# Sparse attention: items in the order of token halves, half of the second key search between the first items, four-head output banks

## The chip, the cores and the metric

The kernel runs on one core of a Trainium2 chip. The metric is the device time of one execution in microseconds (us). The core has TensorE (matrix products, PE), VectorE (DVE), ScalarE (ACT), GpSimd (POOL) and SyncE (SP, which here only issues DMAs), each with its own queue of instructions, worked off in order. They meet on semaphores. TensorE writes to eight PSUM banks of 128 x 512 float32; the others read them from there.

## The reference

Two model blocks run one after the other over 256 tokens of width 1024, all in float32. The first block is a pair of layers (recurrent mixers, then full attention, each with a feed-forward part). The second has, beside a convolution and a pooling branch, a sparse attention with compressed keys, and then a mixture of 32 experts. The sparse attention is what the change touches, cut to its core:

```python
topk = min(TOPK_MAX, S // 4)                       # 64 keys of 256
q_abs = einsum('bthd,khd->bthk', q, w_uk)          # 8 heads, latent width 128
score = einsum('bqhs,bqh->bqs', relu(qi @ ki), wi) * idx_scale
score = where(key_chunk <= query_chunk, score, -inf)   # chunks of 64 tokens
_, idx = top_k(score, topk)                        # the same keys for all heads
logits = einsum('bqhc,bqkc->bqhk', q_abs, ckv[idx]) * att_scale
p = softmax(where(valid, logits, -inf))
ctx = einsum('bqhk,bqkc->bqhc', p, ckv[idx])       # then times w_uv, into y_att
mix = concat([y_conv, y_att, y_pool]) @ w_out
```

## The kernel before, in words

Tokens are split into two halves of 128 (t = 0 and 1), which lie on the 128 partitions. Queries of half t see (t + 1) key blocks of 128: one for the first half, two for the second. Instead of gathering the chosen keys, the kernel builds a bias (0 for a chosen key, -1e30 for the rest) and runs the attention densely over the key blocks.

**The search for the best keys** is on VectorE (`best_keys(t)`, lines 2172 to 2179). It scales and masks the scores into `work` (line 2174), then runs eight rounds of MAX8 (line 2177, the eight greatest values of each row) and MATCH_REPLACE8 (line 2178, which strikes them out), and last turns what was struck out into the bias `bias2` (line 2179). `step` is a wait of VectorE for its own last instruction. Both halves are searched before the attention starts, t = 0 first.

**The attention** works on 16 items, each one head and one half of the tokens. Item i is head i // 2, half i % 2: the halves alternate. An item passes through the engines like this, each engine with its own loop over i, written out by hand:

- TensorE (`attend`, lines 1327 to 1345): the score matmul of item i (line 1334), into a bank of its own; LAG = 4 items later the transposes of its probabilities (line 1341, carried out at line 796), into another bank; and after the transposes of an odd item of head h, the output products of head h - 1 (`out_of`, line 1356), both halves. Two heads share a bank.
- VectorE (`attend`, lines 2034 to 2054): scale and add the bias while reading the bank (line 2044), the negative maximum (line 2047), and two items later the reciprocal of the sum (line 2052) and the product with it (line 2054).
- ScalarE (`attend`, lines 2495 to 2519): the exponential of item i with its row sum (line 2502), then for item i - 4 the copy of the transposed probabilities to `probT2` (line 2514), one of four buffers. It first waits until the output products of the item that had the buffer are done. After items 5, 9 and 13 it also copies a full output bank to `ctxT` (line 2287), and the fourth at the end.

The same functions serve the full attention of the first block ("att"), which the change leaves as it is.

**Banks** are taken in a fixed rotation over the eight (`Banks.take`, line 133); a bank that is held is left out of it until it is released. A taken bank makes TensorE wait until its last content was read. During the sparse attention two banks are held by `out_early(0, 0)` and `out_early(0, 1)`, the parts of the output projection that don't need the attention (lines 1494 to 1509), issued just ahead of it; `out_early(1, 0)` stands right behind it in TensorE's queue.

**What follows:** the products with w_uv (line 1525, "yatt"), whose end frees the slot of the attention's weights and lets SyncE load the first five expert weight units (lines 2677 to 2679); the rest of the output projection, the router, the choice of experts, and the expert stage, whose 96 weight units of 2 MB each pass through eight slots; a slot is loaded anew when TensorE has used it (line 2673).

## Time and profile before

| | us |
|---|---|
| median of 3 runs | 1467.24 |
| lowest and highest run | 1466.57, 1469.61 |
| the profiled execution | 1473.01 |
| its span (first to last instruction) | 1471.2 |
| TensorE busy (matmul) | 1223.2 |
| VectorE busy | 609.4 |
| ScalarE busy | 445.2 |
| first item of the sparse attention begins (line 2044) | 937.73 |
| its last probabilities are ready | 957.49 |
| first expert weights are requested | 965.97 |
| first expert matmul | 1009.85 |

The times in the timeline are microseconds from the span's start, in the profiled execution. A row of the timeline gives the start, the duration, the engine, the line, the operation, what it writes and reads, how many instructions were merged, and in brackets how long the engine had been idle before it and what ended the wait. A float32 matmul shows as two records, so `x2` is one product of one key block. "PEld" are the weight loads beside TensorE's matmuls. The granted clock is TensorE's, as a share of 2.4 GHz. In a row of the stages the count behind a busy time (x12) is its number of instructions.

### The profile page before, as it was taken

To read this page: it belongs to the slowest core of one execution; us is meant where nothing else is said; L and a number is where in the kernel's file an instruction comes from. 1 tells how busy PE (TensorE), PEld (TensorE's weight loads), DVE (VectorE), ACT (ScalarE), POOL (GpSimd) and SP (SyncE) were. 2 spreads that over 40 slices of the span, in tenths; PEclk is the share of its full clock that TensorE was granted. 3 is DMA by queue.
4 is the path that set the end of the run, shared out by engine and by line. 5 is a ranking of instruction groups with operands and counts; after the bars stand their busy time and mean duration, and the time that the engine had idled before them with its cause. 6 is when DMAs were issued, how large, how long until landed. Compare 5 with 4: busy or idle time off the path is not lost.

```text
span 1471.2 us, 18072 instructions
## 1 busy us (share of the span) xinstructions
PE 1223.2 (83%) x7648; PEld 898.1 (61%) x7648; DVE 609.4 (41%) x971; ACT 445.2 (30%) x685; POOL 16.2 (1%) x32
## 2 busy tenths in 40 slices
PE   5999999999999998999999999798464665646637
PEld 5998886699787787599888786554121321312213
DVE  4588423577543666366643548822100100101002
ACT  4662330344333675353432523532010010000002
POOL 2000000000000000000000000000000000000000
PEclk9999999999999999999999989998787878868878
DMA  8362559355464544144455634076999999999995
GB/s 265 123 215 72 199 203 340 125 176 193 160 216 144 195 174 168 57 172 172 172 181 190 190 114 145 1 296 267 428 429 429 429 429 428 428 428 428 429 425 238
DMA packets 98060, 362.98 MB, mean 247 GB/s; under 512 B 7193, under 2 KB 10612, under 8 KB 86084
## 3 DMA queue, kind: packets, MB, share of 16 engines
q1 hardware_dynamic: 95952, 357.70, 62.9%
q0 software_dynamic: 1680, 4.10, 1.0%
q8 instruction: 55, 0.90, 0.2%
q10 hardware_dynamic: 356, 0.13, 0.0%
q14 instruction: 17, 0.14, 0.0%
HBM read 360.87 MB, written 1.05 MB: 246 GB/s over the span
## 4 chain that ended last, share of the span: by engine, by line
PE 59%; DMA 22%; DVE 8%; issue 2%; ACT 2%; SPq 1%; DVEq 0%; ACTq 0%
PE bank L855 33%; DMA arena<-in_exp_w 21%; PE bank L628 7%; PE bank L969 3%; PE bank L796 2%; DVE arena L2123 2%; PE bank L1189 2%; PE bank L827 2%; PE bank L1181 1%; PE bank L1490 1%; PE bank L1162 1%; PE bank L837 1%; SPq L2673 1%; DVE low_w L1636 1%; DMA ring<-in_w_out_ar 1%
## 5 line engine op out<-in xcount | busy, mean ns | idle before, releaser
L628 PE MATMUL bank<-arena 128*32 128x512 f32 x944 | 198.7, 706 | 97.0 <-DMA arena<-in_exp_w 92.1
L1636 DVE TENSOR_TENSOR low_w<-ring,split_high 128x2048 fp32r<-128x2048 f32 x84 | 189.7, 2289 | 114.9 <-ACT split_high L2302 114.8
L855 PE MATMUL bank<-turned_high,low_w 128*128 128x256 f32 x720 | 204.4, 284 | 0.0
L2302 ACT ACTIVATE split_high<-ring 128x2048 fp32r<-128x2048 f32 x84 | 157.6, 1912 | 146.5 <-DMA ring<-in_w_down 60.0
L628 PE MATMUL bank<-ring,arena 128*32 128x512 f32 x528 | 94.0, 694 | 86.6 <-DMA arena<-in_exp_w 86.6
L628 PEld LDWEIGHTS bank<-arena 128*32 128x32 f32 x944 | 51.4, 127 | 167.7 <-issue 167.7
L855 PE MATMUL bank<-turned_high,split_high 128*128 128x256 f32 x512 | 145.9, 285 | 3.0 <-DVE turned_low L1651 3.0
L855 PE MATMUL bank<-turned_low,split_high 128*128 128x256 f32 x512 | 144.9, 283 | 0.0
L855 PEld LDWEIGHTS bank<-turned_high,low_w 128*128 128x128 f32 x720 | 139.0, 193 | 0.0
L733 DVE TENSOR_TENSOR arena<-arena,bank 128x512 f32<-128x512 f32 x8 | 5.5, 689 | 300.1 <-PE bank L628 300.1
L2287 ACT ACTIVATE arena<-bank 128x512 f32<-128x512 f32 x110 | 62.3, 596 | 207.2 <-PE bank L855 135.6
L628 PEld LDWEIGHTS bank<-ring,arena 128*32 128x32 f32 x528 | 26.5, 125 | 150.6 <-issue 150.6
L855 PE MATMUL bank<-split_high,actT_high 128*128 128x512 f32 x256 | 101.3, 396 | 5.3 <-DVE actT_low_late L1964 5.3
L855 PEld LDWEIGHTS bank<-turned_high,split_high 128*128 128x128 f32 x512 | 98.3, 192 | 3.9 <-issue 3.9
L855 PE MATMUL bank<-low_w,actT_high 128*128 128x512 f32 x256 | 100.6, 393 | 0.0
L855 PEld LDWEIGHTS bank<-turned_low,split_high 128*128 128x128 f32 x512 | 98.3, 192 | 0.5 <-issue 0.5
L768 ACT ACTIVATE arena<-bank 128x512 f32<-128x512 f32 x8 | 4.8, 597 | 258.4 <-PE bank L628 258.4
L855 PE MATMUL bank<-split_high,actT_low 128*128 128x512 f32 x192 | 75.9, 395 | 0.0
L855 PE MATMUL bank<-low_w,turned_high 128*128 128x512 f32 x176 | 69.1, 393 | 0.0
L855 PE MATMUL bank<-split_high,turned_high 128*128 128x512 f32 x160 | 64.1, 400 | 3.6 <-DVE low_w L1636 2.1
L855 PE MATMUL bank<-turned_high,split_high_in 128*128 128x256 f32 x208 | 60.6, 291 | 4.0 <-DVE low_w L1636 4.0
L855 PE MATMUL bank<-split_high,turned_low 128*128 128x512 f32 x160 | 63.0, 394 | 0.0
(424 smaller groups left out, 1967.6 us busy)
## 6 DMA issues: line engine op xcount, KB each, us to landing
arena<-in_exp_w SPq DMA_DIRECT2D x59, 2048.0 KB, 22.9
ring<-in_exp_w SPq DMA_DIRECT2D x33, 2048.0 KB, 20.7
ring<-in_w_up SPq DMA_DIRECT2D x16, 2048.0 KB, 8.6
ring<-in_w_down SPq DMA_DIRECT2D x16, 2048.0 KB, 7.9
ring<-in_mod_w SPq DMA_DIRECT2D x12, 2048.0 KB, 8.0
ring<-in_w_in_ar SPq DMA_DIRECT2D x7, 2048.0 KB, 8.6
ring<-in_w_qkv SPq DMA_DIRECT2D x6, 2048.0 KB, 8.0
ring<-in_ple_gate SPq DMA_DIRECT2D x4, 2048.0 KB, 7.9
```

Source lines behind the costliest of these rows:

```text
L628: last = mm(mb[bank][strip(e), :], act[:, k, strip(e)], w[e][:, k, cols], start=(k == 0), stop=(k == n_k - 1), skip_group_check=True)
L796: last = nc.tensor.transpose(dst, src, ident[0:src.shape[0], 0:src.shape[0]])
L827: last = mm(bank.ap[:, i * S:(i + 1) * S], w[:, k, m:m + P], act[:, k, :], start=(k == 0), stop=(k == kcs - 1))
L837: last = mm(bank.ap[:, 0:n], act[:, k, t * P:(t + 1) * P], w[:, k, 0:n], start=(k == 0), stop=(k == kcs - 1))
L855: last = mm(dst, *pair, start=(start and i == 0), stop=(stop and i == 2))
L969: last = mm(bank.ap[:, :], hT3[:, k, t * P:(t + 1) * P], w[:, k, :], start=(k == 0), stop=(k == KC - 1), skip_group_check=True)
L1162: last = mm(mod_bank.ap[strip, :], cond3[:, k, at:at + STRIP], w[:, k, :], start=(c == 0 and k < 4), stop=(c == MOD_UNITS - 1 and k >= 4), ...
L1189: last = mm(bank.ap[:, i * P:(i + 1) * P], a_inv[:, 4 * g + i, :], invT[:, 4 * g + i, :], start=True, stop=True)
L1636: v.tensor_tensor(low_of(name, s), half_of(slot(name), name, s), high_of(name, s).bitcast(F32), ALU.subtract).then_inc(sem("split_low"), 1)
L2123: last = v.scalar_tensor_tensor(conv_acc[:, c, :], src, conv_col[:, c, k:k + 1], conv_acc[:, c, :], ALU.mult, ALU.add)
L2287: s.activation(dst, src, func, scale=scale).then_inc(bank.freed, 1)
L2302: nc.scalar.activation(high_of(name, s), half_of(slot(name), name, s), ACT.Copy)\
```

## The change

- The items of the sparse attention are taken in the order of token halves: items 0 to 7 are the eight heads of half 0 (one key block each), items 8 to 15 those of half 1 (two key blocks each).
- VectorE searches half 0 as before, then masks half 1 and runs four of its eight rounds. The other four stand one each between the maximum and the reciprocal of items 0 to 3, and the bias of half 1 behind the last of them.
- TensorE issues the output product of one item behind the transposes of the next one, in place of a head's two behind the next head's. An output bank holds four heads of one half, in place of two heads of both; it is held (left out of the rotation) from its first product to its last.
- ScalarE copies an output bank, now four heads of one half of `ctxT`, ahead of the transposed probabilities of items 5, 9 and 13 in place of behind them, and the fourth at the end. It waits for single items' output products.

```diff
--- before.py
+++ after.py
@@ -1344,6 +1344,42 @@
                             out_of(tag, h - 1, value, probsT)
                 out_of(tag, HEADS - 1, value, probsT)
 
+            def attend_halves(tag, items_q, items_k, value, landed_sem, probs, probsT):
+
+                n = 2 * HEADS
+
+                def out_item(j):
+                    t, h = divmod(j, HEADS)
+                    if h % 4 == 0:
+                        open_bank[tag] = banks.hold(pe, tag, "o", j // 4)
+                    bank = open_bank[tag]
+                    banks.wait_read(pe, tag, "pT", j)
+                    for k in range(t + 1):
+                        last = mm(bank.ap[:, (h % 4) * P:(h % 4 + 1) * P], value(h, k), probsT[:, j % 4, k, :],
+                                  start=(k == 0), stop=(k == t))
+                    if h % 4 == 3:
+                        last.then_inc(bank.full, 1)
+                        banks.release(tag, "o", j // 4)
+                    else:
+                        last.then_inc(sem(tag + "_out"), 1)
+
+                for i in range(n + LAG):
+                    if i < n:
+                        t, h = divmod(i, HEADS)
+                        bank = banks.take(pe, tag, "s", i)
+                        mm(bank.ap[:, 0:(t + 1) * P], items_q(h)[:, t * P:(t + 1) * P], items_k(h)[:, 0:(t + 1) * P],
+                           start=True, stop=True).then_inc(bank.full, 1)
+                    if i >= LAG:
+                        i2 = i - LAG
+                        t = i2 // HEADS
+                        bank = banks.take(pe, tag, "pT", i2)
+                        pe.wait_ge(sem(landed_sem), i2 + 1)
+                        transposes([(bank.ap[:, k * P:(k + 1) * P], probs[:, i2 % 8, k * P:(k + 1) * P])
+                                    for k in range(t + 1)], bank)
+                        if i2:
+                            out_item(i2 - 1)
+                out_item(n - 1)
+
             open_bank = {}
 
             def out_of(tag, h, value, probsT):
@@ -1510,7 +1546,7 @@
             for g in range(4):
                 banks.wait_read(pe, "qabs", g)
             banks.wait_read(pe, "ckvT")
-            attend("dsa", lambda h: q_abs[:, h, :], lambda h: ckvT, lambda h, k: ckv_tok[:, k, :],
+            attend_halves("dsa", lambda h: q_abs[:, h, :], lambda h: ckvT, lambda h, k: ckv_tok[:, k, :],
                    "dsa_prob", prob2, probT2)
             out_early(1, 0)
             for c in range(4):
@@ -2031,11 +2067,15 @@
                     .then_inc(sem("rotated"), 1)
                 dve.wait_ge(sem("rotated"), q + 1)
 
-            def attend(tag, scale, mask, probs, extra=None):
+            def attend(tag, scale, mask, probs, first_half_first=False, beside=None):
                 n = 2 * HEADS
+
+                def half_of_item(i):
+                    return i // HEADS if first_half_first else i % 2
+
                 for i in range(n + 2):
                     if i < n:
-                        t = i % 2
+                        t = half_of_item(i)
                         bank = banks.read(dve, tag, "s", i)
                         if i >= 8:
                             banks.read(dve, tag, "pT", i - 8)
@@ -2045,9 +2085,11 @@
                             .then_inc(bank.freed, 1)
                         banks.wait_read(dve, tag, "s", i)
                         v.tensor_reduce(nmax[:, i:i + 1], part, AX.X, ALU.max, negate=True).then_inc(sem(tag + "_max"), 1)
+                    if beside:
+                        beside(i)
                     if i >= 2:
                         i2 = i - 2
-                        t = i2 % 2
+                        t = half_of_item(i2)
                         dve.wait_ge(sem(tag + "_exp"), i2 + 1)
                         step(v.reciprocal(rinv[:, i2:i2 + 1], rsum[:, i2:i2 + 1]))
                         part = probs[:, i2 % 8, 0:(t + 1) * P]
@@ -2169,14 +2211,25 @@
                     last.then_inc(sem("rel_used"), 1)
                     dve.wait_ge(sem("rel_used"), 4 * t + g + 1)
 
-            def best_keys(t):
+            def mask_keys(t):
                 n = (t + 1) * P
                 step(v.scalar_tensor_tensor(work[:, t, 0:n], score[:, t, 0:n], float(512) ** -0.5,
                                             c_("allowed", t * S, t * S + n), ALU.mult, ALU.add))
-                for r in range(8):
-                    step(v.max(top8, work[:, t, 0:n]))
-                    step(v.match_replace(work[:, t, 0:n], top8, work[:, t, 0:n], -3e38))
+
+            def next_best(t):
+                n = (t + 1) * P
+                step(v.max(top8, work[:, t, 0:n]))
+                step(v.match_replace(work[:, t, 0:n], top8, work[:, t, 0:n], -3e38))
+
+            def key_bias(t):
+                n = (t + 1) * P
                 step(v.tensor_scalar(bias2[:, t, 0:n], work[:, t, 0:n], -2e38, NEG, ALU.is_gt, ALU.mult))
+
+            def search_beside(i):
+                if i < 4:
+                    next_best(1)
+                if i == 3:
+                    key_bias(1)
 
             add_scores(0)
             bank = banks.read(dve, "cvar")
@@ -2185,9 +2238,14 @@
             dve.wait_ge(sem("conv_root"), 1)
             step(v.reciprocal(conv_m[:, 0, :], conv_m[:, 0, :]))
             v.tensor_tensor(conv_acc, conv_acc, mid(conv_m[:, 0, :], 2), ALU.mult).then_inc(sem("conv_normed"), 1)
-            for t in range(NT):
-                best_keys(t)
-            attend("dsa", 64.0 ** -0.5, lambda t: bias2[:, t, 0:(t + 1) * P], prob2)
+            mask_keys(0)
+            for r in range(8):
+                next_best(0)
+            key_bias(0)
+            mask_keys(1)
+            for r in range(4):
+                next_best(1)
+            attend("dsa", 64.0 ** -0.5, lambda t: bias2[:, t, 0:(t + 1) * P], prob2, True, search_beside)
             for n in range(2):
                 for t in range(NT):
                     bank = banks.read(dve, "w_out2", n, t)
@@ -2518,6 +2576,35 @@
                             evacuate(dst[:, 2 * c:2 * c + 2, :], ACT.Copy, tag, "o", c)
                 evacuate(dst[:, 6:8, :], ACT.Copy, tag, "o", 3)
 
+            def attend_halves(tag, probs, probsT, dst):
+                n = 2 * HEADS
+
+                def take_out(c):
+                    evacuate(dst[:, 4 * (c % 2):4 * (c % 2) + 4, c // 2 * P:(c // 2 + 1) * P], ACT.Copy, tag, "o", c)
+
+                for i in range(n + LAG):
+                    if i < n:
+                        t = i // HEADS
+                        part = probs[:, i % 8, 0:(t + 1) * P]
+                        act.wait_ge(sem(tag + "_max"), i + 1)
+                        s.activation(part, part, ACT.Exp, bias=nmax[:, i:i + 1], accum_out=rsum[:, i:i + 1])\
+                            .then_inc(sem(tag + "_exp"), 1)
+                    if i >= LAG:
+                        i2 = i - LAG
+                        t = i2 // HEADS
+                        if i2 >= 4:
+                            last_item = i2 - 4
+                            if last_item % 4 == 3:
+                                banks.read(act, tag, "o", last_item // 4)
+                            else:
+                                act.wait_ge(sem(tag + "_out"), last_item + 1 - (last_item + 1) // 4)
+                        if i2 >= 5 and (i2 - 5) % 4 == 0:
+                            take_out((i2 - 5) // 4)
+                        bank = banks.read(act, tag, "pT", i2)
+                        s.activation(probsT[:, i2 % 4, 0:t + 1, :], blocks(bank.ap[:, 0:(t + 1) * P], t + 1), ACT.Copy)\
+                            .then_inc(bank.freed, 1)
+                take_out(3)
+
             feed_forward(0)
             act.wait_ge(sem("ple_added"), 2 * NT)
             norm(3, blocks(page(6, 2), NT))
@@ -2606,7 +2693,7 @@
                 bank = banks.read(act, "qabs", g)
                 h0 = 4 * (g % 2) + g // 2
                 s.activation(q_abs[:, h0:h0 + 3:2, :], blocks(bank.ap, 2), ACT.Copy).then_inc(bank.freed, 1)
-            attend("dsa", prob2, probT2, ctxT)
+            attend_halves("dsa", prob2, probT2, ctxT)
             for g in range(2):
                 rows_ = slice(64 * g, 64 * g + 64)
                 for c in range(2):
```

## Rows read from the trace of the kernel before

**Rows 1.** The page: its head, and part 4, the chain that ended last.

```profile
span 1471.2 us, 18072 instructions
...
PE 59%; DMA 22%; DVE 8%; issue 2%; ACT 2%; SPq 1%; DVEq 0%; ACTq 0%
```

**Rows 2.** Stages: length; busy us of PE, PEld, DVE, ACT, POOL; PEclk; DMA share; GB/s.

```profile
940.00:944.00 4.00, 3.82 (x12) 2.48 (x13) 3.76 (x16) 2.30 (x11) 0.00 (x0) 0.50 0.00 0
...
946.00:958.00 12.00, 8.26 (x62) 7.13 (x62) 9.11 (x36) 7.78 (x30) 0.00 (x0) 1.00 0.01 3
...
1008.00:1020.00 12.00, 10.15 (x76) 3.14 (x80) 0.00 (x0) 0.60 (x1) 0.00 (x0) 0.74 0.02 5
...
1025.00:1440.00 415.00, 236.33 (x1666) 95.49 (x1662) 34.99 (x98) 22.75 (x45) 0.00 (x0) 0.79 1.01 428
```

**Rows 3.** Timeline, VectorE, second half's search: start us, us, engine, line, operation.

```profile
929.53 0.43 DVE L2177 MAX8 small<-arena 128x8 f32<-128x256 f32 x1
...
937.40 0.29 DVE L2179 TENSOR_SCALAR arena<-arena 128x256 f32<-128x256 f32 x1
```

**Rows 4.** Timeline, TensorE around the first score matmuls.

```profile
927.15 7.13 PE L1490 MATMUL bank<-ring,hT 128*128 128x512 f32 x16
...
934.12 1.69 PE L1334 MATMUL bank<-arena 128*128 128x128 f32 x10
...
940.18 0.45 PE L796 MATMUL bank<-const,arena 128*128 128x128 f32 x1 [4.36 <-DVE arena L2054]
```

**Rows 5.** Timeline, VectorE: item 2 (narrow) and item 3 (wide).

```profile
939.04 0.28 DVE L2044 SCALAR_TENSOR_TENSOR arena<-bank,arena 128x128 f32<-128x128 f32 x1
...
939.56 0.15 DVE L2052 RECIPROCAL small<-small 128x1 f32<-128x1 f32 x1
...
939.95 0.42 DVE L2044 SCALAR_TENSOR_TENSOR arena<-bank,arena 128x256 f32<-128x256 f32 x1
...
940.74 0.15 DVE L2052 RECIPROCAL small<-small 128x1 f32<-128x1 f32 x1
...
941.19 0.28 DVE L2044 SCALAR_TENSOR_TENSOR arena<-bank,arena 128x128 f32<-128x128 f32 x1
```

**Rows 6.** Timeline, from item 9's start to item 11's.

```profile
946.91 0.42 DVE L2044 SCALAR_TENSOR_TENSOR arena<-bank,arena 128x256 f32<-128x256 f32 x1
...
947.81 0.51 ACT L2502 ACTIVATE arena<-arena,small 128x256 f32<-128x256 f32 x1 [0.52 <-DVE small L2047]
...
948.32 0.36 ACT L2514 ACTIVATE arena<-bank 128x256 f32<-128x256 f32 x1
...
948.58 0.58 ACT L2287 ACTIVATE arena<-bank 128x512 f32<-128x512 f32 x1
...
949.39 0.60 PE L1334 MATMUL bank<-arena 128*128 128x256 f32 x2
...
950.02 0.42 DVE L2044 SCALAR_TENSOR_TENSOR arena<-bank,arena 128x256 f32<-128x256 f32 x1 [0.87 <-PE bank L1334]
```

**Rows 7.** Timeline, item 8 (narrow), its score at the low clock.

```profile
945.32 0.64 PE L1334 MATMUL bank<-arena 128*128 128x128 f32 x2
...
945.99 0.29 DVE L2044 SCALAR_TENSOR_TENSOR arena<-bank,arena 128x128 f32<-128x128 f32 x1 [0.39 <-PE bank L1334]
...
946.64 0.40 ACT L2502 ACTIVATE arena<-arena,small 128x128 f32<-128x128 f32 x1 [0.60 <-DVE small L2047]
...
947.04 0.26 ACT L2514 ACTIVATE arena<-bank 128x128 f32<-128x128 f32 x1
```

**Rows 8.** Timeline, item 15 and the end of the attention.

```profile
955.30 0.42 DVE L2044 SCALAR_TENSOR_TENSOR arena<-bank,arena 128x256 f32<-128x256 f32 x1 [0.87 <-PE bank L1334]
...
958.03 1.68 PE L1356 MATMUL bank<-arena 128*128 128x128 f32 x12
...
959.54 3.60 PE L1490 MATMUL bank<-ring,hT 128*128 128x512 f32 x8
...
965.97 2.42 SPq L2673 DMA_DIRECT2D arena<-in_exp_w  x4
```

## The prediction

> **What bounds the kernel now.** I read the page first: the span is 1471.2 us, and the chain that ended last is TensorE for 59% and DMA for 22% [rows 1]. The stage table shows why both matter. From 1025 us on, the DMA engines are full at 428 GB/s with the expert weights, so that stretch has a fixed length; from 1008 to 1020 us they carry nothing, because all eight weight slots are full and the first group has not been consumed [rows 2]. So the end is set by when routing and the first expert matmuls happen, and every microsecond by which the sparse attention ends sooner or later goes through to the end one to one. The first expert loads wait too for the last use of its weights: they go out at 965.97 [rows 8]. Both move together, so nothing absorbs a delay.
>
> Inside the attention, VectorE is the pacemaker. It searches the keys of the second half in eight rounds of 0.98 us, from 929.53 to the bias at 937.40 [rows 3], and then runs 16 items. An item with one key block (narrow) takes 0.91 us from start to start, one with two (wide) 1.24; up to the reciprocal, the part that items 0 and 1 consist of, it is 0.52 and 0.79 [rows 5]. The first 15 would need 0.52 + 0.79 + 7 x 0.91 + 6 x 1.24 = 15.1 us; item 15 starts 955.30 - 937.73 = 17.57 us after item 0 (937.40 + 0.29 + 0.04) [rows 3, 8]. The missing 2.4 us are three waits for a score matmul: 0.39 us at 945.99, and 0.87 at 950.02 and at item 15 [rows 6 to 8].
>
> **Search moved.** The same 16 + 16 search instructions run, in the same order for each half, and each is one long dependent chain with no hole that other work could fill: rounds are worth 0.98 us wherever they stand. VectorE's total is unchanged. What the move does is reach the first item four rounds and the bias earlier: 937.73 - 4 x 0.98 - 0.33 = 933.47. But TensorE is then still in its 16 early output matmuls and starts the first score only at 934.12 [rows 4]. With 0.45 us for a narrow score (0.67 at the low clock [rows 7], less 0.11 for each of its two records at the full one) item 0 starts at 934.57: a new wait of **+1.1 us**, which the rounds covered before. It can't be nothing (the score's start is fixed by TensorE's own queue) and at most 1.3.
>
> **Order of items.** Narrow items come first. Item 4 starts after 2 x 0.52 + 2 x 0.91 of items and 4.27 of search: 941.70. Without any wait item 15 would start at 934.57 + 4.27 + 15.06 = 953.90, 1.4 us before the 955.30 of now (15.06: two of 0.52, six of 0.91, two of 0.79 + 0.39 = 1.18, five of 1.24). It will not, for a wait that the new code adds. Before, the output products of a head ran one head behind, so that score k+3 waited for what follows the exponential of item k, and only every second one. Now TensorE's order is score i, transposes of i-4, output of item i-5; the last waits for ScalarE's copy of the transposes i-5, and ScalarE issues that copy behind the exponential of item i-1. Score i+1 is queued behind it. So **score k+2 waits for the exponential of item k**, a loop over two items:
> - Narrow, low clock: item start to exponential 0.65, to copy 0.40 [rows 7]; copy 0.26 and 0.1 to TensorE; two output records, 0.126 each by the twelve between 958.03 and 959.54 [rows 8], doubled, 0.50; score 0.67. Sum 2.58 where VectorE needs 1.82.
> - Wide, full clock: 0.90 to the exponential, 0.51 to the copy [rows 6], 0.46 copy and hand-over, output 0.50 (0.25 and 0.36 for a narrow item), score 0.63: 3.00, or 2.65, where VectorE needs 2.48.
> - At items 9 and 13 ScalarE takes the output bank first (0.58 [rows 6], 0.5 start to start), and now ahead of the copy: 3.15 and 3.50.
>
> The clock: it is 0.50 from 940 to 944 and 1.00 from 946 [rows 2]; before it fell TensorE had stood idle from 935.8 to 940.18 [rows 4]. In the new order its five first scores end near 935.2 and the first probability comes near 939.5, so the same idle gap and the same fall; I take the rise at item 8, a little later, since TensorE is less dense. Adding up: item 6 starts at 941.70 + 2.58 = 944.28 (0.76 late), item 8 at 946.9 (between 946.6 with the clock up and 947.3 with it down; 0.8 late), 10, 11, 13, 14 and 15 lose 0.29, 0.44, 0.17, 0.35 and 0.67. Sum of waits 3.5: item 15 starts at 957.4, **+2.1 us** against 955.30. This term holds the 1.1 of the start and the 2.4 us of old waits that go. Bounds: -1.4 (no wait at all) and +3.0 (low clock until item 12).
>
> **Output banks and the end.** Four-head banks, still four, same 0.6 us evacuations. The bank rotation is what changes: two banks are held by the early output, and one more while it is filled, so five rotate. Counting takes through, transposes of item 13 land on the bank of output 2 (items 8 to 11). That bank is full after output 11, which waits for the copy of transposes 11, which stands behind exponential 15. From item 15's start: copy at +1.41, output 11 from +1.87 to +2.37, evacuation to about +3.05, and then TensorE still has transposes 13, 14, 15 and outputs 12 to 15: 6 + 16 = 22 records at 0.112 to 0.126 = 2.5 to 2.8 us. The early output of (1, 0) starts at +5.6 to +5.9; now it starts at 959.54 - 955.30 = +4.24 [rows 8], because transposes ran ahead of that evacuation. **+1.3 us**, the lower end, since the second-last outputs already overlap. Bounds: -0.1 (22 records for 23, were there no bank wait) and +1.7. Behind it the 3.6 us of early output cover the last evacuation as before.
>
> The head products, routing and expert stage are untouched, and a later last use of the weights only moves the loads. SP's queue and the one of GpSimd issue nothing new. Semaphore counts (15 increments in place of 4) cost no time on an engine that waits anyway. Sum: 2.1 + 1.3 = 3.4 us. The profiled execution took 1473.0 (span 1471.2 and 1.8 around it) and the median of the runs is 1467.24; the stage has no part that differs between runs, so I add the same 3.4 us to the median: **1470.6**.
>
> A rule weighed: from 940 to 946 TensorE works at 1.2 GHz and from 946 at 2.4, though it still pauses (8.3 of 12 us busy) [rows 2]. The Trainium skill, TensorE: Matmul & The Clock Gate, section "A second HAM failure mode: psum-queue depth-cycling", says that short idle pauses of a TensorE cycling through PSUM banks can make its clock swing between the levels. By that rule the new, more evenly broken queue could stay at 1.2 GHz for most of the stage. The trace of before agrees only in part: with 3.7 us of pauses in the 12 after 946 its clock did not fall.
>
> **Rivals.**
> - *The clock stays low longer.* TensorE's pauses are shorter but more frequent. Two-item loop for a wide item over a narrow one at 1.2 GHz: 0.90 + 0.51 + 0.36 + 0.50 + 1.06 (0.63 and twice the 0.22 that a narrow score loses) = 3.3. Low until item 12: item 15 at 958.3, +3.0, and the end +1.4: 1467.2 + 4.4 = 1471.6; through the end, 22 records double, 1474.4. For: 940 to 946 is such a time; against: the clock rose in the midst of the same kind of work.
> - *Only one of the two delays is there.* ScalarE's copy reaches TensorE in time (loop below 1.82 and 2.48), or output 11 is early enough to free the bank: about +1.5, 1468.8, no change. Against: the loop's terms are all rows.
> - *Faster.* VectorE alone is the pacemaker and the old bank waits simply go. It decides if an output product can start within about 0.9 us of the item's start: then item 15 starts at 953.9, and the end is 1.4 + 0.1 earlier: 1465.7. For: the two 0.87 us waits come from a bank that is reused six takes later, and the held bank ends that; against: evacuation still stands in ScalarE's queue ahead of work that scores need.
> - *It does not do what it says:* the search's second half lies "between" items but on the same engine, so nothing is hidden; the rest (start +1.1, old waits -2.4 or kept) gives -1.3 to +1.1. Its middle is 1467.2; it shares the mark of "only one delay".
>
> **Chances.** Forecast (both delays, +2.0 to +4.6, 1469.2 to 1471.8) 0.55; clock low longer 0.12; one or no delay near zero net 0.21; faster 0.12. A change of under 0.2% (2.9 us) can't be told from none here: the three runs before lie 3.0 us apart. The forecast sits just above that line, so about 0.6 of it counts as slower: 0.55 x 0.6 + 0.12 + a rest of 0.02 = 0.47 slower. Of "faster" even the bound of all waits gone is 1.5 us, so only 0.07 goes past the line, for what I did not see; 0.46 for no change. Range 1466.0 to 1473.0: it takes in the small cases near 1467 and 1468.8, most of the low-clock case, and leaves out the faster end and the low clock to the end.
>
> **What would show it.** Item 0 of the second search waits about 1.1 us for a score; VectorE's waits for scores grow from 2.1 us in 3 places to about 4.5 in eight or more, on even and odd items; item 15 starts near 957.4; TensorE waits about 0.7 us for ScalarE's last-but-one output evacuation before transposes 13; the early output (1, 0) starts near 963, and the first expert load near 969.4; expert stage unchanged in length. Wrong if the first expert load goes out before 967, if outputs wait for no copy, or if the stage moved and the end did not.

## The result and the profile after

| | before | after |
|---|---|---|
| median, us (20 runs each) | 1469.03 | 1474.11 |
| ratio after / before | | 1.0035 (95%: 1.0027 to 1.0042) |
| profiled execution: time, span | 1473.01, 1471.2 | 1472.86, 1471.1 |

The change makes the kernel slower by 0.35%, that is by 5.1 us (4.0 to 6.2). One of the 20 runs of after took 1843 us at a mean granted clock of 0.66, against 0.92 in the others, and is left out of the ratio. The two profiled executions don't show this in their spans: the one of after reached the attention 4.0 us earlier, in code that is the same, and such differences between executions are as large as the effect. So I read the stage, not the span. "Stage" is from VectorE's scaling of the convolution, the 128x512 product just ahead of the first key search, to the first expert load. This is one profile for each kernel:

| us | before | after | difference | forecast |
|---|---|---|---|---|
| scaling of the convolution to item 0 | 15.59 | 12.47 | -3.12 | -3.2 |
| item 0 to item 15 | 17.57 | 23.70 | +6.13 | +5.3 |
| item 15 to early output (1, 0) | 4.24 | 6.22 | +1.98 | +1.3 |
| early output (1, 0) to first expert load | 6.43 | 6.42 | 0 | 0 |
| **stage** | 43.83 | 48.81 | **+4.98** | +3.4 |

The first two lines belong together, since 4.27 us of search moved from the one to the other. The stage's 5.0 us agree with the 5.1 of the time, as well as single profiles can show it: from the first expert load to the end of the span the two profiles have 505.2 us before and 504.1 after, in code that the change leaves as it is.

VectorE's timeline of after, the first score wait and the items that waited most (the columns as in [rows 5]). It answers to [rows 3 to 5]:

```profile
929.05 0.41 DVE L2222 MATCH_REPLACE8 arena<-small,arena 128x256 f32<-128x256 f32 x1
...
930.64 0.29 DVE L2084 SCALAR_TENSOR_TENSOR arena<-bank,arena 128x128 f32<-128x128 f32 x1 [1.18 <-PE bank L1370]
...
931.17 0.42 DVE L2221 MAX8 small<-arena 128x8 f32<-128x256 f32 x1
...
940.44 0.29 DVE L2084 SCALAR_TENSOR_TENSOR arena<-bank,arena 128x128 f32<-128x128 f32 x1 [0.76 <-PE bank L1370]
...
943.48 0.42 DVE L2084 SCALAR_TENSOR_TENSOR arena<-bank,arena 128x256 f32<-128x256 f32 x1 [0.97 <-PE bank L1370]
...
954.34 0.42 DVE L2084 SCALAR_TENSOR_TENSOR arena<-bank,arena 128x256 f32<-128x256 f32 x1 [0.53 <-PE bank L1370]
```

Item 0 waits 1.18 us: the search that used to cover TensorE's early output matmuls is gone from there. A round stands between two instructions that had nothing to wait for. Items 6, 8, 9, 11, 14 and 15 wait for their scores. The waits of after, from 925 to 967 us (engine, line, what it waited for: us, times, longest), where before had 2.1 us in three places:

```profile
DVE arena L2084 <- PE bank L1370: 4.5, 7, 1.2
...
PE bank L1358 <- ACT arena L2604: 2.8, 5, 0.9
...
PE bank L796 <- ACT arena L2345: 1.9, 3, 0.8
```

The reason is one step back, in TensorE's and ScalarE's rows around items 13 and 15. They answer to [rows 6]:

```profile
950.83 0.42 DVE L2084 SCALAR_TENSOR_TENSOR arena<-bank,arena 128x256 f32<-128x256 f32 x1
...
951.75 0.51 ACT L2590 ACTIVATE arena<-arena,small 128x256 f32<-128x256 f32 x1 [0.57 <-DVE small L2087]
...
952.25 0.58 ACT L2345 ACTIVATE arena<-bank 128x512 f32<-128x512 f32 x1
...
952.73 0.37 ACT L2604 ACTIVATE arena<-bank 128x256 f32<-128x256 f32 x1
...
952.88 0.44 PE L796 MATMUL bank<-const,arena 128*128 128x128 f32 x2 [0.45 <-ACT arena L2345]
...
953.16 0.71 PE L1358 MATMUL bank<-arena 128*128 128x128 f32 x4
...
953.70 0.60 PE L1370 MATMUL bank<-arena 128*128 128x256 f32 x2
```

Read it from item 13 on: exponential at 951.75, then the output bank (L2345) at 952.25, then the copy (L2604) at 952.73, TensorE's transposes at 952.88, output at 953.16, and only behind it the score of item 15 (L1370) at 953.70. VectorE takes it at 954.34, 3.51 us after item 13's start at 950.83. Two wide items need 2.48.

The end of the attention, which answers to [rows 8]:

```profile
955.25 0.51 ACT L2590 ACTIVATE arena<-arena,small 128x256 f32<-128x256 f32 x1 [1.00 <-DVE small L2087]
...
955.76 0.64 ACT L2604 ACTIVATE arena<-bank 128x256 f32<-128x256 f32 x2
...
956.17 0.71 PE L1358 MATMUL bank<-arena 128*128 128x128 f32 x4 [0.94 <-ACT arena L2604]
...
956.98 0.60 ACT L2345 ACTIVATE arena<-bank 128x512 f32<-128x512 f32 x1 [0.59 <-PE bank L1358]
...
957.63 0.44 PE L796 MATMUL bank<-const,arena 128*128 128x128 f32 x2 [0.75 <-ACT arena L2345]
...
960.56 3.60 PE L1526 MATMUL bank<-ring,hT 128*128 128x512 f32 x8
...
966.98 2.61 SPq L2760 DMA_DIRECT2D arena<-in_exp_w  x4
```

The copy of transposes 11 stands behind exponential 15; output 11 follows at 956.17, its bank is evacuated from 956.98, and TensorE's next transposes (item 13) wait 0.75 us for it, with four items of output still to do.

The granted clock of after, and the expert stretch, in the same columns as [rows 2]:

```profile
935.00:945.00 10.00, 7.01 (x24) 5.26 (x24) 7.39 (x32) 3.72 (x17) 0.00 (x0) 0.51 0.00 0
...
946.00:958.00 12.00, 8.11 (x49) 5.97 (x48) 8.60 (x29) 7.49 (x25) 0.00 (x0) 1.00 0.01 2
...
1025.00:1440.00 415.00, 240.41 (x1666) 96.54 (x1662) 35.01 (x98) 22.73 (x45) 0.00 (x0) 0.78 1.01 428
```

The clock is at half from 935 to 945 us; before, it was from 940 to 946. The expert stretch still runs at 428 GB/s, and from the first expert matmul to the end of the span the profiles have 461.4 us before and 460.3 after.

### The profile page after: what moved, and what is told of

Read it like the earlier page. It is cut to its first block, busy times and chain, and to the rows that moved or that the text cites. A ratio compares the mean times of both kernels' runs of the same rounds, so it can differ in the third digit from the quotient of the medians.

```text
span 1471.1 us, 18076 instructions
## 1 busy us (share of the span) xinstructions
PE 1224.2 (83%) x7648; PEld 897.1 (61%) x7648; DVE 609.8 (41%) x971; ACT 445.2 (30%) x685; POOL 16.1 (1%) x32
## 4 chain that ended last, share of the span: by engine, by line
PE 60%; DMA 22%; DVE 7%; ACT 2%; issue 2%; SPq 1%; DVEq 0%; ACTq 0%
PE bank L855 32%; DMA arena<-in_exp_w 21%; PE bank L628 7%; PE bank L969 3%; PE bank L796 2%; PE bank L1526 2%; DVE arena L2165 2%; PE bank L827 2%; PE bank L1189 2%; PE bank L1162 2%; PE bank L1181 1%; PE bank L837 1%; SPq L2760 1%; DVE low_w L1672 1%; DVE arena L2084 1%
## 5 line engine op out<-in xcount | busy, mean ns | idle before, releaser
L628 PE MATMUL bank<-arena 128*32 128x512 f32 x944 | 201.8, 713 | 94.6 <-DMA arena<-in_exp_w 90.2
L2345 ACT ACTIVATE arena<-bank 128x512 f32<-128x512 f32 x110 | 62.2, 596 | 207.7 <-PE bank L855 135.7
```

Of the source, the lines that this page charges most:

```text
L628: last = mm(mb[bank][strip(e), :], act[:, k, strip(e)], w[e][:, k, cols], start=(k == 0), stop=(k == n_k - 1), skip_group_check=True)
L2345: s.activation(dst, src, func, scale=scale).then_inc(bank.freed, 1)
```

## The experiments

All are variants of after but one. "Time" is the ratio of the runs to those of before on the same chip, with its 95% interval; "first matmul" is from the first expert load to the first expert matmul. Stage, waits and first matmul come from one profile of each kernel, the time from 11 or 12 runs of it (20 for after), so the two need not agree to the microsecond. The time of x4 lies lower than its stage says (1.4 us above before would be 1.0010), and no run shows why.

| kernel | stage, us | VectorE's score waits behind item 0 | first matmul | time |
|---|---|---|---|---|
| before | 43.83 | 2.13 | 43.9 | |
| after | 48.81 | 3.29 | 43.8 | 1.0035 (1.0027 to 1.0042) |
| x1 search ahead | 47.28 | 3.05 | 47.3 | 1.0025 (1.0013 to 1.0037) |
| x2 copy first | 44.01 | 0.41 | 45.5 | 1.0016 (1.0003 to 1.0030) |
| x3 evacuation last | 49.05 | 3.58 | 44.0 | 1.0034 (1.0021 to 1.0048) |
| x4 output later | 45.23 | 0.92 | 43.9 | 0.9998 (0.9989 to 1.0007) |
| y1 turn banks | 48.82 | 3.26 | 43.9 | 1.0043 (1.0030 to 1.0056) |
| y2 gap busy | 48.82 | 3.35 | 43.8 | 1.0031 (1.0012 to 1.0050) |
| y3 combined | 43.19 | 0.49 | 43.8 | 0.9998 (0.9982 to 1.0014) |
| y4 combined, gap used | 40.60 | 1.21 | 44.3 | 0.9980 (0.9965 to 0.9994) |
| z1 ahead, busy | 48.22 | 2.69 | 44.1 | 1.0020 (1.0008 to 1.0031) |
| z2 before, gap used | 43.14 | 3.47 | 44.0 | 1.0003 (0.9990 to 1.0016) |
| z3 gap used, search between | 40.92 | 1.33 | 45.6 | 0.9990 (0.9979 to 1.0000) |
| z4 ahead, real filler | 48.27 | 2.69 | 44.0 | 1.0028 (1.0016 to 1.0040) |

### x1: the whole search ahead of the items

```diff
-            for r in range(4):
+            for r in range(8):
                 next_best(1)
-            attend("dsa", ..., prob2, True, search_beside)
+            key_bias(1)
+            attend("dsa", ..., prob2, True)
```

> Stage = from VectorE's scaling of the convolution (the 128x512 product just ahead of the first key search) to the first expert load: 43.8 us before, 48.8 after. Here the new order and banks stay, and all eight rounds of the second search run ahead of the attention. Theory A (score k+2 waits for what follows exponential k; late bank at the end; 1.2 us wait for the first score): only the 1.2 us of the start go, the rest stays: stage 47.6, time 3.9 us above before. Theory C (the search between the items is what costs, since it delays first exponentials and lengthens TensorE's idle time): stage below 46. Theory D (the move hides something): stage above 48.8.

Measured: stage 47.28, 1.53 us less than after (theory A: 1.2), and 3.45 more than before. Theory A holds: the move of the search costs the wait for the first score and hides nothing. Theory C is out: with the search back in its place most of the loss stays, in items that wait as before (0.76, 0.89, 0.30, 0.27, 0.30, 0.53) and the same 6.2 us at the end.

### x2: ScalarE copies ahead of its exponentials

```diff
                 for i in range(n + LAG):
+                    if i >= LAG:
+                        ...            # copy of item i - LAG and output bank
                     if i < n:
                         ...            # exponential of item i
-                    if i >= LAG:
-                        ...
```

> ScalarE copies the transposes (and output bank) of item i-4 ahead of the exponential of item i; all else as after. Theory A: this cuts both the two-item loop and the end (copy 11 no longer behind exponential 15). VectorE's waits for scores fall from 3.5 us behind the first one to about 1.5 (those at the low clock), the end from 6.2 us behind item 15's start to about 4.5; stage about 45, time 0.5 to 1.5 above before. Theory B (TensorE at the low clock with one product per item is simply too slow): waits stay above 3, stage 47.5 or more.

Measured: stage 44.01; behind item 0 only item 8 still waits (0.41 us, where 1.5 in all was expected), and the end is 5.23 us behind item 15's start (expected 4.5). So this one swap takes back 4.8 of the 5.0 us, 3.8 between items 0 and 15 and 1.0 at the end; I had expected 3.8 in all. This is the cleanest sign for the loop, since TensorE's work, order and banks are untouched. The clock is not quite: it was at half for some 7 us here (934 to 940) and for 10 in after, so that item 9's score ran at the full clock. But item 6 lies in the low stretch in both and waits 0.76 us in after and not at all here; and in y2 below the low stretch is 7 us too and the stage as long as after's. ScalarE's rows of this kernel, around item 13:

```profile
946.72 0.58 ACT L2345 ACTIVATE arena<-bank 128x512 f32<-128x512 f32 x1
...
947.20 0.37 ACT L2598 ACTIVATE arena<-bank 128x256 f32<-128x256 f32 x1
...
947.47 0.50 ACT L2604 ACTIVATE arena<-arena,small 128x256 f32<-128x256 f32 x1
...
949.05 0.42 DVE L2084 SCALAR_TENSOR_TENSOR arena<-bank,arena 128x256 f32<-128x256 f32 x1
```

The output bank (946.72) and the copy (947.20) now run before the exponential of item 13 (947.47), which waits for nothing on VectorE's side, and item 15 starts at 949.05 without a wait. In the time the gain is smaller than in the stage (ratio 1.0016); in the profile TensorE's clock fell early in the routing stretch, of which more below.

### x3: output banks 0 and 1 behind the copies

```diff
-                        if i2 >= 5 and (i2 - 5) % 4 == 0:
+                        if i2 == 13:
                             take_out((i2 - 5) // 4)
                         ...            # copy of item i2
+                        if i2 in (5, 9):
+                            take_out((i2 - 5) // 4)
```

> ScalarE takes output banks 0 and 1 behind the copies of items 5 and 9 as before, in place of ahead of them; bank 2 stays ahead. Theory A: items 11 and 15 wait up to 0.5 us less each: stage 48.0. Theory B: no difference (48.8).

Measured: 49.05, 0.24 more, where 48.0 was expected. This part of theory A fell. Items 11 and 15 wait 0.63 and 0.70 us, more than after's 0.51 and 0.53. The score needs both: the bank (the transposes of items 6 and 10 land on it) and the copy. Turning the two around makes the bank later by a copy.

### x4: output products one item later

```diff
-                        if i2:
-                            out_item(i2 - 1)
+                        if i2 >= 2:
+                            out_item(i2 - 2)
+                out_item(n - 2)
                 out_item(n - 1)
```

(and ScalarE takes an output bank at i2 = 6, 10, 14)

> TensorE issues the output product of item j behind the transposes of item j+2 (in place of j+1), and ScalarE takes an output bank one item later. Theory A: the loop becomes three items long and no longer binds; waits of VectorE for scores fall to about 1.6 us (low clock, and 0.4 for a bank at item 12), the end to about 5.4 us behind item 15's start; stage about 46, time 2 above before. Theory B: as TensorE does the same work, the waits stay: 48 or more.

Measured: 45.23 (theory A: about 46), waits 0.92 us in two places (item 8 at the low clock, item 12 for a bank), and 5.86 us at the end. Theory B expected 48 with the same work on TensorE. With x2 this settles the loop: it goes when either of its two links is given room, the product issued an item later or the copy ahead of the exponential.

### y1: banks of the x transposes

Behind the attention the new rotation gives the first transposes of x the bank of output part (1, 0), which VectorE has still to read. After, from TensorE's timeline:

```profile
980.99 0.69 DVE L2253 TENSOR_TENSOR arena<-bank,arena 128x512 f32<-128x512 f32 x1 [2.02 <-PE bank L1526]
...
981.73 1.09 PE L796 MATMUL bank<-const,x 128*128 128x128 f32 x8 [0.85 <-DVE arena L2253]
```

```diff
+            banks.at = 7
             turn_x(0, 0)
             turn_x(0, 1)
```

> As after, but the rotation is set so that the transposes of x behind the output projection take banks 0 and 1 again, as before the change (after, they take the bank of output part (1, 0), and TensorE waits 0.85 us for VectorE to read it). Stage = from VectorE's scaling of the convolution to the first expert load (43.8 before, 48.8 after); next stretch = from the first expert load to the one behind the last piece of the output projection (22.8 before, 23.85 after). Theory A (four places of loss, this one 1.1 us): stage 48.8 unchanged, next stretch 22.8, time about 1 us under after, 4 above before. Rival (that wait lies beside other work): next stretch falls, but the first expert matmul stays at 43.8 us behind the first load, and the time does not change.

Measured: the stretch to the eighth load falls from 23.85 to 22.78 us as expected, but the first expert matmul stays at 43.88 behind the first load and the time does not fall. The rival holds: this wait lies beside other work. What it lies beside is DMA. First expert matmuls of after and of y1:

```profile
1010.76 8.51 PE L628 MATMUL bank<-arena 128*32 128x512 f32 x64 [4.47 <-issue]
```

```profile
1009.20 8.49 PE L628 MATMUL bank<-arena 128*32 128x512 f32 x64 [5.66 <-issue]
```

The eighth load took 19.9 us from 990.83 in after, 21.1 from 988.10 in y1 and 21.0 from 988.75 in before, so it landed at 1010.7, 1009.2 and 1009.8; the matmuls began at 1010.76, 1009.20 and 1009.85. The eighth unit lands 43.8 to 43.9 us behind the first request in all three, and in x1 and x2 too (43.9 and 43.8), whatever routing does meanwhile. So the first matmul follows the first expert load, until routing gets later than that: in x1 the clock fell early in the routing stretch (the row below has length, busy us by engine, clock, DMA; before, it stayed at 1.00 there and was at 0.50 only from 991 to 997, 25 us behind the load), and the first matmul came 47.3 us behind the load; in x2, with the same fall, 45.5. That would explain why x2 gained less in time than in the stage, but only one profile of x2 shows it.

```profile
982.00:992.00 10.00, 9.55 (x36) 6.14 (x35) 0.40 (x1) 2.90 (x7) 0.00 (x0) 0.66 1.02 434
```

TensorE's wait in front of the first expert matmul is shown as "issue". In the code this matmul waits for its own four units (`group_products`), the first to be requested, and not for the eighth; that it starts as the eighth lands is what the profiles show, and why is open.

### y2, z1 and z4: TensorE kept busy in its gap

```diff
+                    if i == LAG:
+                        for _ in range(4):
+                            mm(mixed_bank[(0, 0)].ap[:, :], zeros, const[:, 0:512], start=False, stop=False,
+                               skip_group_check=True)
```

y2 is after with this, z1 is x1 with it; z4 is z1 with real values (features times output weights) into a bank of their own.

> As after, with four products of a zero matrix (added to a held bank, 3.6 us) in TensorE's idle gap between the first five scores and the first transposes; TensorE is then no longer idle for 4.4 us and its granted clock should stay at 1.00. Theory A (loop of two items, made longer by the low clock): VectorE's waits for scores behind the first fall from 3.3 us to about 1.6, those of items 6, 8, 9 nearly vanish, 11, 14, 15 stay; stage 48.8 to about 47. Rival (loop alone, the clock is no part of it): stage stays within 0.3 of 48.8.

> The version with the search ahead of the items (stage from VectorE's scaling of the convolution to the first expert load: 47.28) and four products of a zero matrix in TensorE's gap. In the version with the search between, the same filler did not hold the clock: it fell in the pauses of 1.7 and 0.9 us between the thin first items. If those pauses are the reason, the clock now stays at 1.00 to the end of the attention, VectorE's waits for scores fall from 3.05 us to about 2 (only the loop at the full clock), stage about 46.2. Rival (products of zeros do not count as activity): clock falls as before, stage 47.3.

> The same as the version with the search ahead and a filler of zeros in TensorE's gap (stage 48.2, granted clock low from 937 to 940 and again at the end of the attention), but the four filler products take real values (normed features times output weights) into a bank that nobody reads, with the rotation set back; same sizes, same number. If what the products hold matters to the granted clock, it stays at 1.00 from the gap to the end, VectorE's waits for scores are those of the loop at the full clock (about 2 us, against 2.7) and the stage is 45.7 to 46.4. If only time matters, all is as with zeros: 47.5 or more and a fall within 5 us of the filler's end.

Measured, y2: stage 48.82, nothing gained, and neither theory right about why. The filler ended at 935.8; the clock stayed at 1.00 until 940 and was then 0.51 to 0.50 until 946, so that items 6, 8 and 9 met it as before (0.77, 0.97, 0.22). The filler only moved the fall. z1 and z4 have dense first items, and the clock fell still (from 937 in z1, from 939.5 in z4), so that z1 ended above both values expected of it (46.2 and 47.3). The stages of z4 (length, busy us of PE, PEld, DVE, ACT, POOL, clock, DMA):

```profile
932.00:936.00 4.00, 3.93 (x13) 1.67 (x11) 3.71 (x14) 0.50 (x2) 0.00 (x0) 1.00 0.00 0
...
936.00:939.50 3.50, 1.18 (x7) 0.89 (x8) 3.22 (x16) 2.39 (x10) 0.00 (x0) 1.00 0.00 0
...
939.50:942.50 3.00, 3.00 (x13) 2.38 (x13) 1.98 (x9) 1.70 (x9) 0.00 (x0) 0.53 0.00 0
...
942.50:955.00 12.50, 9.26 (x51) 6.46 (x49) 9.98 (x34) 7.27 (x27) 0.00 (x0) 0.98 0.01 3
...
957.00:960.00 3.00, 3.00 (x15) 3.00 (x15) 0.00 (x0) 0.77 (x2) 0.00 (x0) 0.50 0.00 0
```

TensorE is busy 1.18 of the 3.5 us ahead of the fall. The low time is shorter than in x1, which brings 0.4 us in the items (waits 2.69 against 3.05), but the clock falls a second time at the end and costs 1.4 us there (item 15 to the early output 7.6 us against 6.2). Zeros and real values gave the same to 0.05 us. So the expectation that the gap of 4.4 us is what lowers the clock fell three times: without it the clock falls too, only later. Nor is it a single pause: from the filler to the fall z4 paused 1.09, 0.39 and 0.91 us, while y4 below paused 1.07, 0.39, 1.48 and 1.40 us and stayed at 1.00 through all items. What decides is open. And the loop costs its waits also at the full clock: items 10 to 15 of z4 wait 1.40 us at 0.98 to 1.00.

### y3 and y4: a version from the findings

y3 is x1, x2 and y1 together. y4 puts early output (1, 0), which stood behind the attention, into the gap as well:

```diff
+                    if i == LAG:
+                        out_early(1, 0)
...
-            out_early(1, 0)
```

> After, with the whole search ahead of the items, ScalarE's copies ahead of its exponentials, and the banks of the x transposes set back. Theory A: the single effects add: 48.8 less 1.5 (search) less 4.8 (copies) = stage 42.5, next stretch 22.8 at the full clock; 1.3 us below before, time 0 to 1.5 below before. Rival (waits overlap, so that single gains do not add): stage 43.5 or more.

> As the combined one, and the early part (1, 0) of the output projection (3.5 us of TensorE) is moved from behind the attention into TensorE's idle gap ahead of the first transposes. Theory A: the gap of 4.4 us shrinks to about 1, the clock stays at 1.00, and at the end only 0.8 us for the last output bank remains of the 3.5: stage 42.5 - 2.7 - 0.4 = about 39.5, time about 4 below before. Rival (three held banks starve the rotation): VectorE's waits grow by 2 us or more and the stage stays above 41.

Measured, y3: 43.19, 0.6 us below before, where 42.5 was expected. Of x1's 1.5 us only 0.8 came on top of x2. The time is that of before (0.9998). y4: 40.60, 3.2 us below before, and the time 0.9980 (0.9965 to 0.9994): faster than both kernels. The clock stayed at 1.00 (the expectation came true here, though not in y2, z1 and z4), and TensorE went from the last output product to the products with w_uv in 0.9 us:

```profile
941.38 0.49 PE L1358 MATMUL bank<-arena 128*128 128x128 f32 x2 [1.48 <-ACT arena L2348]
...
942.34 0.42 DVE L2086 SCALAR_TENSOR_TENSOR arena<-bank,arena 128x256 f32<-128x256 f32 x1 [0.56 <-PE bank L1370]
...
954.12 0.60 ACT L2348 ACTIVATE arena<-bank 128x512 f32<-128x512 f32 x1 [0.80 <-PE bank L1358]
...
954.98 2.83 PE L1562 MATMUL bank<-arena,ring 128*64 128x256 f32 x16 [0.89 <-ACT arena L2348]
...
957.84 0.34 SPq L2763 DMA_DIRECT2D arena<-in_exp_w  x1
```

Three held banks do cost: TensorE waited 1.48 us for output bank 0 and 1.40 for the next, and VectorE 0.56 and 0.65 us for scores. That is part of why the gain is 3.2 and not 4.3; the rest is y3's shortfall of 0.7.

### z2: the same use of the gap in the kernel before

> The kernel before, with the early part (1, 0) of the output projection in TensorE's gap ahead of the first transposes and the banks of the x transposes as they were; no item order, no four-head bank. If the gain of the best version so far (stage 40.6, against 43.8 before) comes from that move and not from the new order, this one reaches 40.5 to 41.5. If the held four-head banks and ScalarE's order are needed beside three held banks, VectorE's waits grow (2.1 us before) to 4 or more and the stage stays above 42.5.

Measured: 43.14 and a time as before; the waits, 3.47 us, stayed below the 4 expected. What the move saves at the end (8.6 us from item 15 to the first load, 10.7 before) is mostly lost in two waits of 1.51 us, at items 10 and 14. With five free banks the score itself lands on an output bank that ScalarE has yet to take:

```profile
DVE arena L2046 <- PE bank L1334: 3.5, 3, 1.5
...
PE bank L1334 <- ACT arena L2289: 3.2, 2, 1.7
```

The clock was at half here too, from 940 to 943. So the rest of y4 (item order, held banks, copies ahead of exponentials) is worth 2.5 us beside this move; which of the three it is was not tried.

### z3: the search between the items, without the first wait

y4 with the change's search, and the first five scores issued ahead of early outputs (0, 1) and (1, 0):

> The best version so far (stage 40.6), but with half of the second search between items 0 to 3 as in the change, and the first five scores ahead of the early parts (0, 1) and (1, 0), so that VectorE does not wait for the first score. If the search is worth the same wherever it stands because VectorE is the pacemaker, the stage is 40.6 within 0.5. If spreading it hides something, 39.6 or less. If the thin first items let the clock fall, 41.3 or more.

Measured: stage 40.92, item 0 waited for nothing. The search is worth the same wherever it stands (0.3 us more here, with a short fall of the clock at items 7 to 9). The time is 0.9990 (0.9979 to 1.0000).

## Why the prediction was right and wrong

- **The direction and the causes were right.** Slower, through the wait for the first score, the two-item loop, and a late output bank at the end. Item 0 waits 1.18 us (forecast 1.1). VectorE's waits for scores are 4.5 us in seven places (forecast about 4.5 in eight or more). x1, x2 and x4 each take away the part that the theory gives them, or somewhat more: 1.5, 4.8 and 3.6 us, where 1.2, 3.8 and 2.8 were expected.
- **The predicted time, 1470.6, missed 1474.1 by 3.5 us, and the range ended 1.1 below it.** Half of this is the base, the step "so I add the same 3.4 us to the median": the median of three runs was 1467.24, that of twenty of the same kernel is 1469.03. From there the same sum gives 1472.4, inside the range. The other half is the sum "2.1 + 1.3 = 3.4": 5.1 (4.0 to 6.2) measured, in the profiles +3.0 to item 15 and +1.98 behind it. The +3.0 is the figure of the rival "The clock stays low longer", but not by its way, as the clock rose before item 10.
- **Mis-sized: "I take the rise at item 8".** The scores of both item 8 and item 9 ran at the low clock (0.51 from 935 to 945). From item 4's start, item 9 came after 7.21 us where 6.38 were forecast; that is nearly all of the 0.9 us by which the term for the items was short. (0.1 of it was there at item 6, after 2.68 us for 2.58; the loop to item 8, a wide score at the low clock, took 3.04.) Behind it the loop is as computed: items 11 to 13 took 2.68 us (forecast 2.65), 12 to 14 3.07 (3.00), 13 to 15 3.51 (3.50).
- **Mis-sized: the end, "+1.3 us, the lower end".** The start of output 11 came at +1.83 (forecast +1.87), but its bank was full later, evacuation from +2.64 in place of +2.45, and the 22 records took 0.133 us each, 2.9 us, where I took 2.5. Measured +1.98. To choose the lower end of one's own range for a term in a series of dependent steps had no row behind it.
- **Two claims about clock and order fell.** That the idle gap ahead of the first transposes is what it takes to lower the clock: it fell without the gap in y2, z1 and z4. That the evacuation ahead of the copy costs 0.5 us in the loop: x3. Only the sum of the two was right.
- **"A later last use only moves the loads", right**, and more than I saw: in most profiles the first expert matmul follows the first expert load alone, so that the 1.1 us of the turn bank, which I had not found, cost nothing (y1).
- **One sign misled.** "Wrong if the first expert load goes out before 967": it went out at 966.98, but this profile had reached the stage 4.0 us earlier. By the stage it is 970.95, where 969.4 was forecast. A sign has to be counted from an event of the same profile.
- **The rivals.** "It does not do what it says" is right in its half about the search (x1, z3). "Faster" named the right point, whether an output product can start in time; it can with x2's order, and then the waits go. The clock stayed low longer than forecast, to item 9, but not to item 12. The clock rule of the Trainium skill (TensorE: Matmul & The Clock Gate, A second HAM failure mode: psum-queue depth-cycling), by which short pauses between groups of matmuls can make the clock swing, has more for it than I allowed: z4's clock fell though no pause since the filler was over 1.1 us. But it is not the whole, as y4, with pauses of up to 1.48 us, stayed at 1.00.

## What to carry to other kernels

Where three engines pass items around, write down for each queue what stands directly ahead of the instruction that the next engine needs: a copy behind the next exponential closed a loop over two items here, and turning the two around took back 4.8 us of a 5.0 us loss, although no engine did more work. Moving work between items hides nothing if the engine it runs on is the pacemaker; the place it leaves may have been covering something. A held bank is one that cannot rotate, so count the takes through to see whose reader the next transposes will wait for.

## What the runs showed that I had not expected

- Keeping TensorE busy in one gap of 4.4 us only put off the fall of its granted clock to 0.50: in z4 it stayed at 1.00 through the filler (to 935.9) and the first short bursts behind it, and fell at about 939.5. Products of zeros did the same as real ones. In y4, with early output in the same gap and ScalarE's copies ahead, it did not fall in the attention at all; which difference decides is open.
- In 10 of 14 profiles the first expert matmul came 43.8 to 44.1 us behind the first expert load, whether the eighth unit was requested 22.8 or 23.9 us behind the first. In the other four it was requested 25.5 to 27.2 us behind, and the matmul came after 44.3 to 47.3.
- Executions reach the same instruction at times up to 6.6 us apart (scaling of the convolution at 916.4 to 923.0 us in 14 profiles of kernels that are the same up to there), so that the span of a single profile says nothing on a change of 5 us.
